# Delta stage: raw keys with the norm folded into beta, four more z units on raw activations, new orders

## The reference, cut

```
proj = rmsnorm(h, w) @ w_in                      # q, k, v, z, b, a
qkv = silu(causal_dwconv(qkv, conv_w))           # four taps
q = l2norm(q) * 128 ** -0.5;  k = l2norm(k)
beta = sigmoid(b);  g = -exp(a_log) * softplus(a + dt_bias)
gc = cumsum(g) in each chunk
m = strict_lower((beta * k) @ k.T * exp(gc_i - gc_j));  t = inverse(I + m)
u = t @ (beta * v);  w = t @ (beta * k * exp(gc))
for chunk:  v_new = u - w @ S;  o = (q * exp(gc)) @ S + (lower(q @ k.T) * decay) @ v_new
            S = S * exp(gc_last) + (k * exp(gc_last - gc)).T @ v_new
out = (rmsnorm(o) * silu(z)) @ w_out
```

## Time and profile before

| | |
|---|---|
| median of 3 runs | 1277.47 us (1276.85 to 1277.61) |
| profiled execution, its span | 1277.6 us, 28536 instructions |
| TensorE busy | 1242.6 us, 97% |
| VectorE busy | 910.9 us, 71% |
| ScalarE busy | 777.0 us, 61% |
| GpSimd busy | 249.2 us, 20% |
| Delta stage after its opening | 563.8 to 782.1 us |

### The profile page before, as it was taken

The page is one execution under the profiler, slowest core; times in us unless marked ns, Lnnn a source line. Parts: engine busy times, 40 slices in busy tenths (PEclk is TensorE's granted clock), DMA queues, the critical chain, the costliest instruction groups (busy, mean ns, idle before and its releaser), DMA issues.

```text
span 1277.6 us, 28536 instructions
## 1 busy us (share of the span) xinstructions
PE 1242.6 (97%) x10472; PEld 1212.7 (95%) x10472; DVE 910.9 (71%) x1634; ACT 777.0 (61%) x1287; POOL 249.2 (20%) x226
## 2 busy tenths in 40 slices
PE   7999999999999999997999999999999999999997
PEld 7999999998999999995999989999999889999997
DVE  5866556887787665688877477777766697777654
ACT  5544445598564444567886696666665476666643
POOL 0000000010000000024576100245510231444400
PEclk9999999999999999998999999999999999999999
DMA  7655465464356556644757125765587524666463
GB/s 231 205 173 173 139 171 176 158 198 109 116 182 197 184 145 197 191 146 139 210 152 224 35 67 168 212 192 183 171 206 189 187 75 149 189 186 183 141 196 109
DMA packets 87804, 212.53 MB, mean 166 GB/s; under 512 B 19429, under 2 KB 34085, under 8 KB 87600
## 3 DMA queue, kind: packets, MB, share of 16 engines
q1 hardware_dynamic: 85504, 204.58, 53.1%
q0 software_dynamic: 1664, 6.48, 2.2%
q10 hardware_dynamic: 560, 0.44, 0.1%
HBM read 208.41 MB, written 3.06 MB: 166 GB/s over the span
## 4 chain that ended last, share of the span: by engine, by line
PE 89%; DVE 6%; ACT 2%; issue 1%; DMA 1%; DVEq 0%; ACTq 0%
PE bank L545 20%; PE bank L547 20%; PE bank L546 20%; PE bank L2857 3%; PE bank L2858 3%; PE bank L2859 3%; PE bank L1646 1%; PE bank L2983 1%; DVE wl L413 1%; PE bank L1648 1%; PE bank L1647 1%; PE bank L518 1%; PE bank L522 1%; PE bank L519 1%; PE bank L3494 1%
## 5 line engine op out<-in xcount | busy, mean ns | idle before, releaser
L408 ACT ACTIVATE wh<-raw 128x1024 fp32r<-128x1024 f32 (+3 forms) x423 | 407.4, 970 | 336.7 <-PE bank L547 286.5
L413 DVE TENSOR_TENSOR wl<-raw,wh 128x1024 fp32r<-128x1024 f32 (+3 forms) x364 | 402.6, 1110 | 146.7 <-ACT wh L408 145.8
L545 PE MATMUL bank<-XH,wh 128*128 128x256 f32 (+1 forms) x1448 | 411.5, 284 | 3.4 <-DVE XL L985 3.2
L547 PE MATMUL bank<-XH,wl 128*128 128x256 f32 (+1 forms) x1448 | 410.9, 284 | 0.0
L546 PE MATMUL bank<-XL,wh 128*128 128x256 f32 (+1 forms) x1448 | 410.6, 284 | 0.0
L545 PEld LDWEIGHTS bank<-XH,wh 128*128 128x128 f32 x1448 | 274.1, 189 | 4.4 <-DVE XL L985 3.6
L547 PEld LDWEIGHTS bank<-XH,wl 128*128 128x128 f32 x1448 | 274.4, 190 | 0.0
L546 PEld LDWEIGHTS bank<-XL,wh 128*128 128x128 f32 x1448 | 273.0, 189 | 0.0
L545 PE MATMUL bank<-AH,wh 128*128 128x256 f32 (+1 forms) x704 | 198.6, 282 | 0.0
L547 PE MATMUL bank<-AH,wl 128*128 128x256 f32 (+1 forms) x704 | 198.5, 282 | 0.0
L546 PE MATMUL bank<-AL,wh 128*128 128x256 f32 (+1 forms) x704 | 198.2, 282 | 0.0
(11 more groups left out here) (392 smaller groups left out, 2238.1 us busy)
## 6 DMA issues: line engine op xcount, KB each, us to landing
raw<-in_w_up SPq DMA_DIRECT2D x175, 512.0 KB, 4.3
raw<-in_w_down SPq DMA_DIRECT2D x64, 384.0 KB, 3.4
raw<-in_w_down SPq DMA_DIRECT2D x64, 320.0 KB, 3.2
raw<-in_w_gvz SPq DMA_DIRECT2D x32, 512.0 KB, 4.2
raw<-in_w_gout SPq DMA_DIRECT2D x16, 512.0 KB, 4.8
raw<-in_w_gqk SPq DMA_DIRECT2D x12, 512.0 KB, 4.0
raw<-in_w_mv SPq DMA_DIRECT2D x8, 512.0 KB, 4.5
raw<-in_w_mqk SPq DMA_DIRECT2D x8, 512.0 KB, 5.0
```

The lines of the kernel that those rows point to most:

```text
L408: eng.activation(WH[s][:, 0:n, :], raw[s][:, 0:n, :], ACT.Copy).then_inc(s_hi[s], 1)
L413: eng.tensor_tensor(WL[s][:, 0:n, :], raw[s][:, 0:n, :], WH[s][:, 0:n, :].bitcast(F32), ALU.subtract).then_inc(s_lo[s], 1)
L545: eng.matmul(out, WH[s][:, i, :], xh, start=start, stop=False)
L547: mm = eng.matmul(out, WL[s][:, i, :], xh, start=False, stop=stop)
```

## The change

- Units 4 to 7 are keys (`gk1`), units 8 to 11 z (`gz1`); both multiply raw activations. Queries begin with unit 12, and only from there on gXH and gXL are read. z of `gz1` is multiplied by R on VectorE (`zx`) instead of copied.
- gXS takes turns in banks 4, 2 and 3 of PSUM, and R is copied to bank 5 (`rp`).
- Gates: the half with the decay is kept in PSUM (pA, pE), softplus is summed inside the scan, the rate is applied by ScalarE after it (`gcs`), the memset goes.
- Keys stay raw. Their sums of squares come as columns (16 matmuls with one moving column), beta over the sum (`b2`) takes the norm's place in m, its row (`brow`, `brc`, `bst`) goes to DRAM for the solve, and beta times the inverse root (`lnr`, `exr`, `br`) takes beta's place for v. NBC is made by ScalarE, KC, NB and BR by GpSimd.
- The decays are masked and raised to exp in GCB itself, after `eg(g)`; EG is one buffer for all groups. U is zeroed after at(3), since it shares GCB's place.
- ScalarE loads a table set for exp and log by hand in seven places.
- New orders on every queue. VectorE begins gzs(0), sc(3), sc(1), sc(0), sc(2), gzs(1), taps(0), taps(1), gzs(2), the gates, taps(2), the scans, gzs(3), beta. ScalarE runs hi(12), xh(0), qs(1), xh(4), xh(2), eg(0), xh(5), xh(3), hi(14), eg(2), xh(7), hi(13), sq(1), eg(3), hi(15), xh(6) in a row, and later hi(33), zs(1), hi(35), hi(34), three tap3, hi(36), hi(37), xt. GpSimd has all low halves from 5 to 55 but 14, 15, 38, 48 and 51, with lo(35) ahead of lo(34) and lo(37) ahead of lo(36). `xt` also waits for qd(3), `scatT` goes ahead of `scatU`.

The core of the diff:

```diff
-        gqk1 = stage("gqk1", a["w_gqk"], 3, whole(4), [0, 1, 6, 7], SEQ, XN)
-        gz = stage("gz", a["w_gvz"][1:4, :, 32:64, :], 3, whole(4), [0, 1], SEQ, XN)
+        gk1 = stage("gk1", a["w_gqk"], 1, whole(4), [1, 2, 3, 0], SEQ, X)
+        gz1 = stage("gz1", a["w_gvz"][1:2, :, 32:64, :], 1, whole(4), [1, 6, 7, 0], SEQ, X)
+        gqk1 = stage("gqk1", a["w_gqk"], 2, whole(4), [0, 1, 6, 7], SEQ, XN)
+        gz = stage("gz", a["w_gvz"][2:4, :, 32:64, :], 2, whole(4), [0, 1], SEQ, XN)
...
 
+        def exp_and_log(eng):
+
+            eng.add_instruction(mybir.InstLoadActFuncSet(name=nc.get_next_instruction_name(), act_func_set_id=EXP_LOG))
...
-            def dve(self, eng, product, it=0):
-                d, n = self.dv, GDN_V
-                d.done(eng.memset(dO[:, :], 1.0), "one")
+            def dve(self, eng, product, free, it=0):
+                d, n, b = self.dv, GDN_V, bank[0]
                 self.norm.ready(eng)
                 eng.wait_ge(*product)
-                b = bank[0]
+                eng.wait_ge(*free)
+                d.done(eng.tensor_tensor(pA, b[32:32 + n, 0:SEQ], R[32:32 + n, 0:SEQ], ALU.mult), "a")
                 d.done(eng.tensor_tensor(dB[:, :], b[0:n, 0:SEQ], R[0:n, 0:SEQ], ALU.mult), "b")
-                d.done(eng.tensor_tensor(dA[:, :], b[32:32 + n, 0:SEQ], R[32:32 + n, 0:SEQ], ALU.mult), "a")
                 d.wait(eng, it, "a")
-                d.done(eng.tensor_scalar(dA[:, :], dA[:, :], vec[0:n, VEC["dn"] + 1:VEC["dn"] + 2], None, ALU.add), "x")
-                d.wait(eng, it, "x")
-                d.done(eng.tensor_scalar(dG[:, :], dA[:, :], 0.0, None, ALU.max), "pos")
+                d.done(eng.tensor_scalar(dP[:, :], pA, vec[0:n, VEC["dn"] + 1:VEC["dn"] + 2], 0.0, ALU.add, ALU.max), "pos")
+
+            def dve_beta(self, eng, it=0):
+                d, ac = self.dv, self.ac
+                ac.wait(eng, it, "eb")
+                d.done(eng.tensor_scalar(pE, pE, 1.0, None, ALU.add), "b1")
+                d.wait(eng, it, "b1")
+                d.done(eng.reciprocal(dB[:, :], pE), "beta")
 
             def dve_rest(self, eng, it=0):
                 d, ac = self.dv, self.ac
-                ac.wait(eng, it, "eb")
-                d.done(eng.tensor_scalar(dB[:, :], dB[:, :], 1.0, None, ALU.add), "b1")
-                d.wait(eng, it, "b1")
-                d.done(eng.reciprocal(dB[:, :], dB[:, :]), "beta")
                 ac.wait(eng, it, "ln")
-                d.done(eng.tensor_tensor(dG[:, :], dG[:, :], d2[:, :], ALU.add), "sp")
-                d.wait(eng, it, "sp")
-                d.done(eng.tensor_scalar(dG[:, :], dG[:, :], dE[:, 0:1], -1.0, ALU.mult, ALU.mult), "g")
-                d.wait(eng, it, "g")
+                d.wait(eng, it, "pos")
                 for c in (0, 1):
                     s = slice(c * P, (c + 1) * P)
-                    d.done(eng.tensor_tensor_scan(dA[:, s], dO[:, s], dG[:, s], 0.0, ALU.mult, ALU.add), f"gc{c}")
-
-            def act(self, eng, it=0):
+                    d.done(eng.tensor_tensor_scan(dA[:, s], dP[:, s], pA[:, s], 0.0, ALU.add, ALU.add), f"gc{c}")
...
+            def act_beta(self, eng, free, it=0):
+                self.dv.wait(eng, it, "b")
+                eng.wait_ge(*free)
+                self.ac.done(eng.activation(pE, dB[:, :], ACT.Exp, scale=-1.0), "eb")
+
+            def act_abs(self, eng, it=0):
+                self.dv.wait(eng, it, "pos")
+                self.ac.done(eng.activation(d1[:, :], pA, ACT.Abs, bias=vec[0:GDN_V, VEC["dn"] + 1:VEC["dn"] + 2]), "abs")
+
...
+            def act_log(self, eng, it=0):
+                self.ac.wait(eng, it, "exp")
+                self.ac.done(eng.activation(pA, d1[:, :], ACT.Ln, bias=1.0), "ln")
+
...
             def pool(self, eng, it=0):
-                self.dv.wait(eng, it, "gc1")
+                self.ac.wait(eng, it, "gcs")
                 eng.dma_start(gc_d, dA[:, :]).then_inc(self.ms, 16)
-                eng.dma_start(beta_d, dB[:, :]).then_inc(self.mbeta, 16)
+
+            def pool_spread(self, eng):
                 eng.wait_ge(self.ms, 16)
                 eng.dma_start(GCB[:, :, :], gc_d.partition_broadcast(P)).then_inc(self.mb, 16)
...
-        XS, = carve(big + 40960, 8192, gXS=([P, DC, SEQ], F32))
+        XS = [bank[b][:, 0:SEQ] for b in (4, 2, 3)]
+        RP = bank[5][:, SEQ:2 * SEQ]
+        SS, SE, RR = (bank[5][:, c:c + GDN_V] for c in (64, 80, 96))
+        BROW = bank[5][0:GDN_V, P:3 * P]
...
+                def rp():
+                    eng.wait_ge(*A.past("cols"))
+                    A.done(eng.activation(RP, R[:, 0:SEQ], ACT.Copy), "rp")
...
+                def nbc():
+                    eng.wait_ge(*V.past("bb"))
+                    A.done(eng.activation(NBC[:, :, :], B2[:, :, :].rearrange("p n h -> p h n"), ACT.Copy, scale=-1.0), "nbc")
+
+                def brc():
+                    eng.wait_ge(*T.past("brow"))
+                    A.done(eng.activation(dB[:, :], BROW, ACT.Copy), "brc")
...
+                def lnr():
+                    eng.wait_ge(*A.past("sse"))
+                    A.done(eng.activation(RK[:, :], RK[:, :], ACT.Ln), "lnr")
+
+                def exr():
+                    eng.wait_ge(*A.past("lnr"))
+                    A.done(eng.activation(RK[:, :], RK[:, :], ACT.Exp, scale=-0.5), "exr")
...
                 def xt():
                     eng.wait_ge(*V.past("b30"))
+                    eng.wait_ge(*V.past("qd3"))
                     A.done(eng.activation(XTs[:, :, :], Xs[:, :, :].rearrange("p i c -> p c i"), ACT.Copy), "xt")
...
                 def xs(c):
-                    if c == 0:
-                        self.norm.ready(eng)
-                    V.done(eng.scalar_tensor_tensor(XS[:, c, :], H[:, c, META:TM], gains["ga"][:, c:c + 1], R[:, 0:SEQ],
+                    eng.wait_ge(*A.past("rp"))
+                    if c > 2:
+                        eng.wait_ge(*V.past(f"xl{c - 3}"))
+                    elif c:
+                        self.evicted(eng, 4 + c)
+                    else:
+                        self.gate.dv.wait(eng, 0, "gc1")
+                    V.done(eng.scalar_tensor_tensor(XS[c % 3], H[:, c, META:TM], gains["ga"][:, c:c + 1], RP,
                                                     ALU.mult, ALU.mult), f"xs{c}")
 
                 def xl(c):
                     eng.wait_ge(*A.past(f"xh{c}"))
-                    V.done(eng.tensor_tensor(XNL[:, c, :], XS[:, c, :], XNH[:, c, :].bitcast(F32), ALU.subtract),
+                    V.done(eng.tensor_tensor(XNL[:, c, :], XS[c % 3], XNH[:, c, :].bitcast(F32), ALU.subtract),
                            f"xl{c}")
+
+                def zx(j):
+                    self.unit_done(eng, j)
+                    V.done(eng.tensor_tensor(Z[:, j - 4, :], self.out(j), R[:, 0:SEQ], ALU.mult), f"zx{j}")
...
+                def b2():
...
+                    V.done(eng.tensor_scalar(SE, SS, EPS, None, ALU.add), "se")
+                    eng.wait_ge(*V.past("se"))
+                    V.done(eng.reciprocal(RR, SE), "rr")
+                    eng.wait_ge(*V.past("rr"))
+                    for n in two:
+                        ins = eng.tensor_tensor(B2[:, n, :].rearrange("p (k i) -> p k i", i=2),
+                                                COLS[:, n, 1, :].rearrange("p (k i) -> p k i", i=2),
+                                                RR[:, 8 * n:8 * n + 8].unsqueeze(2).to_broadcast([P, 8, 2]), ALU.mult)
+                    V.done(ins, "bb")
...
+                def br():
+                    eng.wait_ge(*A.past("exr"))
+                    for n in two:
+                        ins = eng.tensor_tensor(BR[:, n, :].rearrange("p (k i) -> p k i", i=2),
+                                                COLS[:, n, 1, :].rearrange("p (k i) -> p k i", i=2),
+                                                RK[:, 8 * n:8 * n + 8].unsqueeze(2).to_broadcast([P, 8, 2]), ALU.mult)
+                    G.done(ins, "br")
...
+                for j in range(28, 30):
                     load(j)
+                load(31)
+                load(33)
+                load(32)
+                load(35)
+                load(34)
+                load(36)
+                load(39)
                 xd()
-                for j in range(37, 40):
-                    load(j)
+                load(37)
                 xtd()
+                load(38)
                 load(40)
+                scatT()
                 scatU()
                 load(41)
...
                 def ss(x):
                     eng.wait_ge(*A.past(f"sq{x}"))
-                    if x == 0:
-                        eng.wait_ge(*A.past("cols"))
-                        self.evicted(eng, 5)
-                    else:
-                        self.evicted(eng, 0)
-                        self.evicted(eng, 1)
-                    for i in two:
-                        sums(x, i, bank[2 + 2 * x + i])
+                    for c in (5, 6, 7):
```

(49 more changed lines are left out.)

824 lines of the change are left out of this document (443 added, 381 removed), and 46 rows, old and new, of the table WP.

## The result

The changed kernel takes **1300.85 us** (median of 4, 1299.45 to 1302.06) against 1277.54 of the kernel before in the same session (4 runs): a ratio of **1.0177, 95% interval 1.016 to 1.0193**. The forecast was 1270 and "faster".

The account below looks back on a forecast made before the run. TensorE, busy nearly throughout with one dip before the middle, was taken to bound the kernel. 15.9 + 0.2 - 2.0 - 4.7 - 1.0 - 0.7 = 7.7 us off 1277.6 gave 1270 us, range 1262.5 to 1275.5.

Parts of the forecast that it names:

- 15.9 us between 563.78 and 596.37: TensorE's waits and low clock in this stretch, around units 4 and 5 and the sums of squares: 15.9 us gained.
- Key sums +0.2: Raw keys' sums of squares as one-column matmuls on TensorE, 2.9 us plus 0.3 for transposes against 3.4: 0.2 us gained.
- -2.0 at the chunks: ScalarE's high parts late for the normed chunks, xl(6) near 593.8: 2 us given back, bounds 0 and 6.
- -4.7 at c1(0): Load and scatter chain through DRAM, 27.4 us against 22.7 of cover: TensorE waits 4.7 us, part at unit 36.
- rival A: All gaps close, waits at c1(0) and chunks under a microsecond; sign: no wait at c1(0). 1263 us, chance 0.21.
- Clock -1.0: Low clock behind the two new gaps, at the chunks and c1(0): 1.0 us lost, bounds 0 and 3.
- -0.7 for everything behind c1(0): Less cover for c1 to c7, fewer table loads, GpSimd's output low halves: 0.7 us lost, bounds 0 and 5.
- Rival C: GpSimd's SBUF reads block VectorE's two-SBUF instructions ahead of xt; slower from six blocks, 1282 us with seven; chance 0.06.
- the 7.7 of the sum: Net gain predicted for the whole kernel, all terms added: 7.7 us.
- B: The first stall only moves to the chunks, ScalarE's parts 4 us later, clock falling again: 1274 us, chance 0.13.
- E: ScalarE's explicit table set is replaced by single ones, seven more loads of 1.28 us: 1273 us, chance 0.06.

Follow-up runs that it names:

- a2_u37: Changed kernel with only the order of loads, high halves and low halves around the scatter (units 36 to 39) repaired: 1301.83 us.
- a3_natural: Changed kernel with loads, high halves and low halves of units 4 to 55 in order of use on SP, ScalarE and GpSimd: 1278.99 us.
- a6_wait: a3_natural with unit quarters spread between c1 and c7, p3b(0) evicted ahead of two high halves, and gq(3) three quarters later: 1280.82 us.
- a1_tail: Changed kernel with only the tail reordered: GpSimd's low halves 52, 53, 54, 55, ScalarE's high half of 54 before 55: 1287.80 us.
- b1_tail: Kernel before, given the changed kernel's tail order, with low halves 53, 52, 55 moved from VectorE to GpSimd behind 54: 1291.14 us.
- a5_late: Changed kernel with natural order for units 34 to 55 only, earlier inversions kept: 1282.83 us.
- a10_nohold: a9_hold without SP's wait before the load of unit 42: median 1278.81 us, ratio to the kernel before 1.0005.
- a9_hold: a6_wait with gq(3) moved back, loads from unit 42 on held until c3(1) (the hold), high half of 42 behind e3(0): median 1274.16 us.

## Why the prediction was wrong, step by step

- **15.9 us between 563.78 and 596.37 given back: right as a mechanism.** TensorE shows no wait from 564 to 586 us, the clock is 1.00, a chunk of gXS takes 0.484 us on average where the earlier trace rows had 5.45 at the worst. The column transposes come at 570.41 without a wait.
- **Key sums +0.2: mis-sized by 0.3 us.** Sixteen records take 1.92 us in the row above (at a clock below 1.00 in part) and 1.70 at 603.36 in a2_u37: 3.4 for both, plus 0.1 for the two transposes, where I took 2.9 and 0.3.
- **-2.0 at the chunks: right in place, low in size.** The waits are 1.52, 0.94, 0.98 and 0.22 us around 588 to 595, 3.7 in all, and the clock is 0.83 from 590 to 600. gk(3) ends at 603.9 where the forecast had it near 598. In a3_natural, with the loads and halves in order, it ends at 600.3: the inversions there were worth 3.6.
- **-4.7 at c1(0), "part of it at unit 36": right chain, wrong victim, and the sum ended too early.** The wait is 5.32 us and all at unit 36; c1(0) has none. The forecast's sign for rival A, no wait at c1(0), came true in a kernel that is 23 us slower. I priced the chain to c1(0) and let the other inversions cost nothing. From the grams to c1(0) 13.3 us went, not 4.7: 5.3 here, 3.8 in four waits of 0.8 to 1.2 at 624, 636, 648 and 652, about 2 at the half clock behind unit 36 (0.50 from 684 to 690), the rest not itemized.
- **Clock -1.0: wrong.** I priced the clock per gap of 2.2 us from the earlier trace rows. In the scatter stage a stop of about 2 us was followed by 10 us (the changed kernel), 14 us (a3_natural) and 20 us (a6_wait) at 0.50. The slow stretch, not the wait, is the price.
- **-0.7 for everything behind c1(0): the step that failed.** It held 16.3 + 2.9 us. I had read that GpSimd "takes most low halves of the output weights", and priced it as contention. I did not walk the order of the last four units as I had walked that of the scatter, nor hi(43) ahead of c4(1). What stood there was a wait of 9.7 us for unit 52's low half, one of 2.3 us in c5(1), and half clock behind both. a1_tail and b1_tail put 13 us on the order of the last four; a3_natural's sorting takes 21.9 in all.
- **Rival C, contention: not the cause in the changed kernel, but next in line.** Of the twelve two-SBUF instructions ahead of xt two were blocked there, for 1.3 us together: one of wb's takes 1.23 us for 0.69, one of qd's 1.13 for 0.41; both kn take 1.22 as before. Beside GpSimd's low halves at the end YL took 3.11 and 2.23 us for 1.21, and XL 2.27 and 2.56 for 0.48. The Trainium skill (SBUF — State Buffer, Who interferes with whom) names this lock; the trace agrees, and TensorE did not wait for it in this kernel. It did once the orders were repaired: 4.2 us behind two blocked qd in a2_u37 and 4.0 in a5_late, and probably the 2.1 to 2.2 us at `at(2)` in a3_natural and most kernels made from it. So this rival's mechanism may hold a part of what lies between the 3.6 us and the 7.7 of the sum; no run took it away. **The other rivals**: A's 1263 was never reached, the lowest single execution is 1269.88 (a10_nohold); the loss did not move to the chunks (B), TensorE is 9.8 us ahead behind them; the table sets stay (E), 15 loads from 560 to 812 us where the kernel before has 21.
- **The total.** Repaired and with the hold, the change gives 3.6 us in the median and up to 6 in its better executions, against the 7.7 of the sum; repaired without the hold it gives nothing in the median.

**What stays open.** That the fetch of instructions is what stops TensorE in c1(1) rests on the packet's place in the profiles above and on the pair a9_hold and a10_nohold; the profile names no releaser for the stop, and a10_nohold's profiled execution has only 0.29 us of it. The hold also keeps the loads away from everything else that runs in 690 to 697, and no run separates that from the fetch. Whether the hold would help the kernel before wasn't tried, so the 3.6 us are those of the change and the hold together.
